# One kernel for two model blocks: eight weight subtractions per mixer moved to GpSimd, and the attention output turned within its own block

## The reference, cut to what matters

```python
def hybrid_mixer(x, w_in, sc_conv_w, attn_sink, cc_conv_w, cc_conv_b, cc_ln_g, cc_ln_b, w_out):
    z = x @ w_in                                   # 512 x 1792
    sc_b, sc_c, sc_h, q, k, v, cc_a, cc_gate = jnp.split(z, IN_OFFSETS, axis=-1)
    y_sc = sc_b * depthwise_conv(sc_c * sc_h, sc_conv_w)            # width 3
    q, k = rope(q), rope(k)                        # 8 query heads, 2 key heads of 64
    y_att = banded_window_attention(q, k, v, attn_sink)             # |distance| <= 128
    u = cc_a * jax.nn.sigmoid(cc_gate)
    u = depthwise_conv(u, cc_conv_w) + cc_conv_b                    # width 31
    y_cc = jax.nn.silu(layer_norm(u, cc_ln_g, cc_ln_b))
    return jnp.concatenate([y_sc, y_att, y_cc], axis=-1) @ w_out
```

## Time and profile before

| | |
|---|---|
| median of 3 runs | 3588.47 us (3584.19 to 3596.56) |
| the profiled execution | 3588.47 us, span 3586.4 us |
| mean granted clock of TensorE | 0.973 |
| attention and convolution stretch of a mixer | 148 us, twice |
| in it, first mixer: busy VectorE, ScalarE, GpSimd | 102.12, 64.91, 0 us |

### The profile page before, as it was taken

The page is one execution under the profiler, slowest core; times in us unless marked ns, Lnnn a source line. Parts: engine busy times, 40 slices in busy tenths (PEclk is TensorE's granted clock), DMA queues, the critical chain, the costliest instruction groups (busy, mean ns, idle before and its releaser), DMA issues. The chain is left out here.

```text
span 3586.4 us, 42414 instructions
## 1 busy us (share of the span) xinstructions
PE 3357.7 (94%) x16776; PEld 2741.2 (76%) x16776; DVE 1725.5 (48%) x2508; ACT 1104.1 (31%) x1619; POOL 146.8 (4%) x204
## 2 busy tenths in 40 slices
PE   6989889989989999999999997999999999989999
PEld 5767777867767777778888766888888887668887
DVE  6645654456644643354332685333443336753334
ACT  5432223333432222223321343332223213423321
POOL 1000000000000000000000101000000000010000
PEclk9999999999999999999999998999999999989999
DMA  5222212222221111132232211233233322123232
GB/s 219 76 78 83 71 60 71 71 92 100 77 85 62 54 47 53 48 106 95 99 107 99 77 36 65 94 100 110 79 101 100 112 89 78 34 71 100 94 112 76
DMA packets 83493, 303.11 MB, mean 85 GB/s; under 512 B 9680, under 2 KB 9952, under 8 KB 83296
## 3 DMA queue, kind: packets, MB, share of 16 engines
q1 hardware_dynamic: 78064, 283.11, 23.5%
q0 software_dynamic: 5232, 17.31, 1.4%
HBM read 295.66 MB, written 4.72 MB: 84 GB/s over the span
## 5 line engine op out<-in xcount | busy, mean ns | idle before, releaser
L553 PE MATMUL bank<-hh,whi 128*128 128x512 f32 (+1 forms) x2704 | 1083.6, 401 | 38.2 <-DVE mrg L1138 11.1
L555 PE MATMUL bank<-hh,wlo 128*128 128x512 f32 (+1 forms) x2704 | 1037.3, 384 | 0.0
L554 PE MATMUL bank<-hl,whi 128*128 128x512 f32 (+1 forms) x2704 | 1035.6, 383 | 0.0
L1138 DVE TENSOR_TENSOR wlo<-raw,whi 128x1024 fp32r<-128x1024 f32 x498 | 610.4, 1226 | 809.2 <-ACT whi L1996 744.2
L1996 ACT CAST whi<-raw 128x1024 fp32r<-128x1024 f32 x498 | 524.2, 1053 | 755.3 <-PE bank L555 696.9
L553 PEld LDWEIGHTS bank<-hh,whi 128*128 128x128 f32 x2704 | 521.6, 193 | 167.9 <-issue 47.7
L555 PEld LDWEIGHTS bank<-hh,wlo 128*128 128x128 f32 x2704 | 519.9, 192 | 98.8
L554 PEld LDWEIGHTS bank<-hl,whi 128*128 128x128 f32 x2704 | 522.1, 193 | 81.1 <-issue 2.7
L553 PE MATMUL bank<-whi,fh 128*128 128x512 f32 x704 | 274.4, 390 | 0.0
L555 PE MATMUL bank<-whi,fl 128*128 128x512 f32 x704 | 273.9, 389 | 0.0
L554 PE MATMUL bank<-wlo,fh 128*128 128x512 f32 x704 | 273.9, 389 | 0.0
(11 more groups left out here) (319 smaller groups left out, 3724.3 us busy)
## 6 DMA issues: line engine op xcount, KB each, us to landing
raw<-in_W SPq DMA_DIRECT2D x514, 512.0 KB, 3.3
bc<-in_ln_g POOLq DMA_DIRECT2D x6, 512.0 KB, 4.0
bc<-in_ln_b POOLq DMA_DIRECT2D x6, 512.0 KB, 5.6
xn<-in_x SPq DMA_DIRECT2D x4, 512.0 KB, 9.4
mrg<-in_W SPq DMA_DIRECT2D x2, 1024.0 KB, 13.0
AR<-in_W SPq DMA_DIRECT2D x2, 1024.0 KB, 17.6
xn<-in_x POOLq DMA_DIRECT2D x4, 512.0 KB, 5.3
xd<-xn POOLq DMA_DIRECT2D x4, 512.0 KB, 3.5
```

The lines of the kernel that those rows point to most:

```text
L553: e.matmul(out, ah, bh, start=first, stop=False, skip_group_check=True)
L554: e.matmul(out, ah, bl, start=False, stop=False, skip_group_check=True)
L555: return e.matmul(out, al, bh, start=False, stop=last, skip_group_check=True)
L1138: return self.e.tensor_tensor(o, a, b, op)
```

## The change

For each mixer:

1. The last eight of the ten convolution units get their low half from GpSimd, in `Pool.mixer`, right after the paddings; VectorE's `halve` skips them (`by_pool`).
2. The input unit `ca` of each half of the wide convolution comes before its gate unit `cgt`, and so ScalarE's sigmoid comes after two units and not after one.
3. The turn of `ao` follows the value products of block (nb, 1) at once, on TensorE, and so do ScalarE's copy and VectorE's subtraction. `turn_ao`, `lower_ao` and `copy_ao` fall away as functions. On ScalarE the copy now stands ahead of the exponentials of block (nb+1, 0).
4. VectorE takes a block's row sums right behind the scaling of the block before it, not one block later.

```diff
@@ TensorE, conv_units
+        self.k.by_pool |= set(range(self.k.n_split + 2, self.k.n_split + 10))
         for j in range(2):
+            yield from self.proj2(("ca", l, j), l, 1536 + j * 128, self.side2)
             yield from self.proj2(("cgt", l, j), l, 1792 + j * 128, self.side2)
-            yield from self.proj2(("ca", l, j), l, 1536 + j * 128, self.side2)
@@ TensorE, scores
-            if i == 2 and kvh and nb:
-                self.turn_ao(l, nb - 1)
@@ TensorE, end of values
+        if kvh:
+            bank = self.bank(self.ps, ("aot", l, nb))
+            self.wait_ge(("aon", l, nb, 1))
+            self.turn(bank, [k.ao[:, i * 128:(i + 1) * 128] for i in range(4)], ("aot", l, nb))
@@ VectorE, halve
+        if i in self.k.by_pool:
+            return
@@ VectorE, attention
             yield from self.scores(l, *at)
-            if at[1] and at[0]:
-                self.lower_ao(l, at[0] - 1)
             if held:
                 yield from self.values(l, *held)
+            self.weights(l, *at)
@@ VectorE, values
-        for i in range(5):
-            if i == 3:
-                self.weights(l, nb, kvh, k0, nk)
+        for _ in range(5):
             yield
...
+        if kvh:
+            v8 = lambda x: x[:, 1024:3072].rearrange("p (j n) -> p j n", j=4)[:, :, nb * 128:(nb + 1) * 128]
+            key = ("aot", l, nb)
+            self.lower(v8(k.xl8), k.bank(key)[:, :].rearrange("p (j n) -> p j n", j=4), v8(k.xh8), [("xah", l, nb)],
+                       [("free", key)] + ([("xl", l, j) for j in range(2, 6)] if nb == 3 else []))
@@ ScalarE, conv_units
         for j in range(2):
             yield from self.steps()
+            yield from self.steps()
             key = ("cgt", l, j)
             self.wait_ge(key, *([("cuu", l, 0)] if j else []))
             self.act(z[0], k.bank(key)[:, :], ACT.Sigmoid).then_inc(*self.up(("cgs", l, j), ("free", key)))
-            yield from self.steps()
@@ ScalarE, attention
-            if at[1] and at[0]:
-                self.copy_ao(l, at[0] - 1)
@@ ScalarE, end of values
+        if kvh:
+            v8 = lambda x: x[:, 1024:3072].rearrange("p (j n) -> p j n", j=4)[:, :, nb * 128:(nb + 1) * 128]
+            key = ("aot", l, nb)
+            self.wait_ge(key)
+            self.e.copy(v8(k.xh8), k.bank(key)[:, :].rearrange("p (j n) -> p j n", j=4)).then_inc(
+                *self.up(("xah", l, nb), *([("xh", l, j) for j in range(2, 6)] if nb == 3 else [])))
@@ Pool, mixer
+        for i in sorted(k.by_pool)[8 * l:8 * l + 8]:
+            hi, lo = k.halves(i)
+            self.wait_raw(k.raw_of[i])
+            self.wait_ge(("hi", i), ("used", i - RING))
+            self.e.tensor_tensor(lo, k.raw_unit(k.raw_of[i]), hi.bitcast(F32), ALU.subtract).then_inc(*self.up(("lo", i)))
```

More of the change, by code:

```diff
@@ L236, in __init__ @@
         self.n_split = 0
+        self.by_pool = set()
         self.sems = {}
@@ L1084, in attention @@
         yield from self.values(l, *held)
[L1085 to L1091, removed]
     def scores(self, l, nb, kvh, k0, nk):
@@ L1936, in attention @@
         yield from self.values(l, *held)
[L1937 to L1944, removed]
     def scores(self, l, nb, kvh, k0, nk):
@@ L2464, in attention @@
         yield from self.values(l, *held)
[L2465 to L2473, removed]
     def weights(self, l, nb, kvh, k0, nk):
```

## The result

The changed kernel takes 3627.22 us (median of 4 runs, 3625.79 to 3638.37) against 3586.33 us for the kernel before in the same comparison: a ratio of 1.0108 (1.0093 to 1.0124). It is slower by 1.1%, with an interval clear of 1, and by nearly three times what was forecast: 40.9 us instead of 14.2.

What follows compares the result with a forecast made beforehand. VectorE was taken to bound the mixers' stretch up to 2139 us. Per mixer, -5.0 - 2.2 - 2.4 + 0.2 + 3.9 + 4.1 + 0.5 + 8.0 = +7.1 us, +14.2 for both: 3602.7 us, range 3575 to 3622.

Steps and rivals of the forecast that it cites:

- Part 1: Eight subtractions move from VectorE to GpSimd: saves 5.0 us of VectorE and a 2.2 us cast wait per mixer.
- part 5: GpSimd's subtractions, taken as 1.9 us, block VectorE's accumulation steps at five places: +8.0 us per mixer, bounds 0 and 13.
- One sign: Expected in the changed profile: VectorE's acc steps show gaps of 1 to 2 us next to GpSimd's subtractions.
- Part 2: Convolution input before gate: later sigmoid delays VectorE's accumulation +0.2 us; TensorE's 1.2 us wait is made good.
- Part 3: Turn and row sums at once: VectorE waits at three block ends, +3.9, +4.1 and +0.5 us; TensorE's stops stay hidden.
- Rival (c): TensorE at half clock after turns ending (1,1) and (2,1): 4 us each on top, +15 a mixer, 3618.6 us; chance 0.15.
- Part 4: With less queued on VectorE, TensorE's stop at 2081.90 and VectorE's 2.43 us wait at 2093.69 vanish: -2.4 us per mixer.
- The sign of being wrong that was named: Forecast is wrong if TensorE, not VectorE, sets the pace between 2055 and 2139 us once the subtractions are gone.
- (a): GpSimd works beside VectorE at no cost, round trips eat the relief: -0.9 us a mixer, 3586.7 us; chance 0.20.
- (b): No exclusion, exponentials done before VectorE's sums at ends of (0,1), (1,1): -7.7 us a mixer, 3573 us; chance 0.15.

Runs made afterwards that it cites:

- e1: Kernel before with only the last eight convolution units' low halves subtracted by GpSimd: -0.7 us per mixer, 3582.71 us, ratio 0.9995.
- e2: Kernel before with only each wide-convolution input unit put ahead of its gate unit: +8.9 us per mixer, 3607.29 us, ratio 1.0057.
- e6: Kernel before with input unit ahead of gate unit, and VectorE copying the input out of its bank at once: +3.6 us per mixer, ratio 1.0018.
- e3: Kernel before with only the turn of ao, its copy and lowering right behind the block's products: +12.0 us per mixer, 3612.65 us, ratio 1.0076.
- e5: Kernel before with ao turned at once, plus 4 and 6 overwritten filler products ahead of the first two turns: -2.3 us per mixer, ratio 0.9999.
- e13: Kernel before with ao turned at once and row sums taken one block earlier, nothing else: +13.8 us per mixer, 3610.18 us, ratio 1.0068.
- e14: Kernel before with ao turned at once, early row sums, and 4 and 6 fillers ahead of the first two turns: +8.5 us per mixer, ratio 1.0050.
- e7: Kernel before plus useless GpSimd subtractions reading SBUF at the eight moments a mixer: +4.5 us per mixer, 3600.18 us, ratio 1.0038.
- e4: Kernel before with only a block's row sums taken by VectorE one block earlier: +1.0 us per mixer, 3591.40 us, ratio 1.0017.
- e11: Kernel before with 3, 2 and 12 filler products at its own three TensorE stops: -0.1 us per mixer, 3584.07 us, ratio 0.9986.
- e8: Kernel before plus useless GpSimd memsets, which only write, at the eight moments a mixer: -0.4 us per mixer, 3586.78 us, ratio 0.9998.

## Why the prediction was wrong, and where it was right

The sign was right, and the size was not: +18.9 us per mixer against +7.1. By its own terms:

- **Part 1 with part 5** was forecast at -7.2 + 8.0 = +0.8 us and measured -0.7 (e1). Right in mechanism and size. GpSimd's subtraction took 2.38 us where 1.9 was taken from the rows (the estimate from the Trainium skill, GPSIMD Engine Reference, 3.1, was 2.3, nearer the truth), and contention came to 8.9 us of busy time in e1, and to 8.8 in the `acc` steps alone of the changed kernel. One sign was misread: it shows as longer `acc` steps (898 ns for 752) and not as gaps between them.
- **Part 2, "+0.2 us", is a step that failed.** The walk for VectorE came out: it began to accumulate 17.9 us after the stretch's start (2049.28 - 2031.4) where before it was 17.7 (2054.86 - 2037.2), just +0.2. But I followed VectorE and ScalarE and held TensorE's stop, put at 1.2 us for a copy, to be made good. I never asked which bank the third unit writes to and who frees it now. It cost 8.9 us by itself (e2), 5.3 of it by the bank (e6).
- **Part 3, "TensorE stands ... and does not become the bound", is the other.** The stops were as foreseen in kind (4 us twice; measured 3.19 and 7.04). What VectorE stands for at the two block ends came out as well: 1.95 us for ScalarE's copy and 2.50 for its exponentials each time, 8.9 us where 3.9 + 4.1 = 8.0 was forecast. To this come 1.95 us at 2100.12, after a block's first half, where nothing was added, and 4.21 in the first block, which costs little. Rival (c) had the mechanism, the half clock behind a stop, and was put aside with "I hold these hidden behind VectorE". e3 and e5 show that premise false: of two engines that wait for each other at every score, one at half pace makes the other late, for as long as the half clock lasts. On the turn alone the half clock costs 14.2 us (e3 less e5), where (c) had 8 on top. With the early sums it costs 5.3 (e13 less e14), since the two losses share their time, and turn and sums together cost 13.8, where parts 3 and 4 had 8.5 - 2.4 = 6.1. e14's 8.5 without the half clock in its long part is not a match for the 8.5 of part 3: it holds the 2.3 that the turn gives.
- **Part 4, "-2.4 us", did not come in the changed kernel.** The wait of 2.43 us at the scaling of `ao` is 1.54 us there. What comes back hung on TensorE being ahead, and it was not. In e5, where the clock stays full, neither that wait nor TensorE's stop of 2.79 us is left: the step was right in kind, and fell with part 3.
- **Right besides:** the rest of the stretch and its 12 us gap didn't move; three subtractions of nine are left on VectorE in the stretch; there are eight table loads for seven; and outside the two stretches the profiled execution, 3622.52 us with a span of 3620.7, is 3.7 us shorter (34.1 more than the earlier trace rows's execution, less 37.8), which is within what other versions vary there. The sign of being wrong that was named, TensorE and not VectorE setting the pace, came in part: VectorE is busy for 70% of the long part, and waits 12.1 us in it for scores.

(a) is out: contention is real, and against what spoke for (a), VectorE's own subtractions are stretched too beside long GpSimd reads (e7). (b) is out: it needed the waits at the two block ends to be under 3.5 us together, and they are 8.9, for the reason given, that ScalarE works in order; e4 shows that the sums would be nearly free without the copy ahead. Open stay what makes up the last 3.6 us of part 2, why parts 1 and 2 cost less together than apart, and the small difference of e11 in total.

## What to carry to other kernels

When two producers are exchanged in order, write down for each rotating buffer who frees it, and after which wait, before summing durations: here the exchange added one table load of 1.28 us on ScalarE to the engines' work and cost 8.9 us. A stop of TensorE that leaves it at the half clock is priced by who needs the products behind it; in e5, where VectorE waited for them, a few products that nobody reads, put ahead of the wait, took 14.2 us off the stretch, and in e11, where nobody was held up by them, they brought nothing. Losses in the same place mask each other, so a part tried alone, or a mend tried alone, tells less than the pair.

## What the runs showed of the hardware

- A VectorE accumulation step with two SBUF inputs that started 0.30 us after a GpSimd subtraction of 128 x 1024 took 2.63 us instead of 0.75, and ended 0.55 us after GpSimd did. The profile shows this as busy time, not as idle time. Where VectorE's step had started first, GpSimd's subtraction was the longer one: 2.88 us at 2102.00 in the changed kernel, against 2.34 to 2.38 for the other four beside the accumulation.
- Moving eight subtractions of 1.23 us a mixer to GpSimd, where each takes 2.38, brought 0.7 us (e1), less than two mixers of one run differ by. Memsets on GpSimd beside the same steps left their mean at 752 ns (e8).
- A stop of 4.17 us left TensorE at 1.2 GHz, with a turn of 1.11 us for 0.66 (e3); four products that nobody reads, ahead of the same wait, kept it at 2.4 GHz, and the stretch was 2.3 us shorter than before (e5).
- A higher granted clock is worth nothing where no engine waits for TensorE's products: 0.88 became 0.95 with 148.1 us both times (e11).
